# The order of small steps in a two-model transformer kernel: the first norm's weight halves, TensorE's order and VectorE's order at the end of the linear attention

## The reference

```
o_g = o_g * lax.rsqrt(jnp.mean(o_g * o_g, axis=-1, keepdims=True) + EPS)
o_g = o_g.reshape(bsz, seq, GLA_V) * gla_g.astype(F32_2) * jax.nn.silu(gr)
...
mu = jnp.mean(o_r, axis=-1, keepdims=True)
var = jnp.mean(jnp.square(o_r - mu), axis=-1, keepdims=True)
o_r = ((o_r - mu) * lax.rsqrt(var + EPS)).reshape(bsz, seq, RET_V)
o_r = (o_r * gn_g.astype(F32_2) + gn_b.astype(F32_2)) * jax.nn.silu(rg)
o = jnp.concatenate([o_g, o_r], axis=-1).astype(h.dtype)
return o @ w_out
```

## Time and profile before

| | |
|---|---|
| median of 3 runs | 2454.0 us (2450.01 to 2458.52) |
| profiled execution | 2458.52 us, span 2457.1 us |
| TensorE busy | 92% of the span |
| VectorE busy | 65% |
| ScalarE busy | 48% |
| DMA, mean over the span | 174 GB/s |

### The profile page before, as it was taken

The page is one execution under the profiler, slowest core; times in us unless marked ns, Lnnn a source line. Parts: engine busy times, 40 slices in busy tenths (PEclk is TensorE's granted clock), DMA queues, the critical chain, the costliest instruction groups (busy, mean ns, idle before and its releaser), DMA issues.

```text
span 2457.1 us, 44886 instructions
## 1 busy us (share of the span) xinstructions
PE 2270.8 (92%) x19011; PEld 2046.4 (83%) x19011; DVE 1602.9 (65%) x2442; ACT 1174.1 (48%) x1703; POOL 0.2 (0%) x4
## 2 busy tenths in 40 slices
PE   7789788999998888889999989999989999999998
PEld 7469788999976787889998989998988888877776
DVE  6537776688773587666776756555765554477886
ACT  5234534455552354344655435444444443456665
POOL 0000000000000000000000000000000000000000
PEclk9999898999999998989998989999988999999999
DMA  5664333355446542334654425563413554579995
GB/s 206 250 237 157 114 103 112 129 198 194 150 172 240 209 145 86 120 111 139 196 199 137 143 64 179 181 185 135 145 35 111 191 182 181 176 271 324 322 327 194
DMA packets 118634, 427.06 MB, mean 174 GB/s; under 512 B 13344, under 2 KB 16160, under 8 KB 118304
## 3 DMA queue, kind: packets, MB, share of 16 engines
q1 hardware_dynamic: 116016, 421.81, 50.0%
q10 hardware_dynamic: 2416, 2.37, 0.3%
HBM read 423.08 MB, written 1.05 MB: 173 GB/s over the span
## 4 chain that ended last, share of the span: by engine, by line
PE 76%; DVE 15%; ACT 5%; issue 3%; DMA 2%; SPq 0%; ACTq 0%; DVEq 0%
PE bank L801 75%; DVE w_low L2276 4%; DVE arena L2308 4%; DMA ring<-in_weights 2%; DVE arena L2317 1%; ACT w_high L1746 1%; DVE y_mix L2308 1%; DVE arena L2813 1%; PE bank L1631 1%; ACT arena L2025 1%; DVE arena L2312 0%; DVE arena L2314 0%; DVE small L2811 0%; DVE arena L2327 0%; ACT arena L1970 0%
## 5 line engine op out<-in xcount | busy, mean ns | idle before, releaser
L2276 DVE TENSOR_TENSOR w_low<-ring,w_high 128x1024 fp32r<-128x1024 f32 x700 | 822.8, 1219 | 156.6 <-ACT w_high L1746 155.8
L1746 ACT ACTIVATE w_high<-ring 128x1024 fp32r<-128x1024 f32 x700 | 699.8, 1051 | 168.8 <-PE bank L801 159.4
L801 PE MATMUL bank<-u_high,w_high 128*128 128x256 f32 x2576 | 740.2, 287 | 29.7 <-DVE u_low L2308 19.7
L801 PE MATMUL bank<-u_low,w_high 128*128 128x256 f32 x2576 | 731.8, 284 | 0.0
L801 PE MATMUL bank<-u_high,w_low 128*128 128x256 f32 x2576 | 731.4, 284 | 0.0
L801 PEld LDWEIGHTS bank<-u_high,w_high 128*128 128x128 f32 x2576 | 496.6, 193 | 43.8 <-issue 35.5
L801 PEld LDWEIGHTS bank<-u_low,w_high 128*128 128x128 f32 x2576 | 496.4, 193 | 0.1
L801 PEld LDWEIGHTS bank<-u_high,w_low 128*128 128x128 f32 x2576 | 495.4, 192 | 0.0
L801 PE MATMUL bank<-arena 64*64 64x64 f32 (+5 forms) x4456 | 240.5, 251 | 77.6 <-issue 20.8
L801 PEld LDWEIGHTS bank<-arena 64*64 64x64 f32 (+2 forms) x4456 | 210.0, 155 | 115.9 <-issue 62.0
L2308 DVE TENSOR_TENSOR arena<-arena 128x256 f32<-128x256 f32 (+3 forms) x218 | 141.7, 666 | 46.7 <-ACT arena L2069 21.3
(11 more groups left out here) (307 smaller groups left out, 3057.9 us busy)
## 6 DMA issues: line engine op xcount, KB each, us to landing
ring<-in_weights SPq DMA_DIRECT2D x534, 512.0 KB, 4.5
ring<-in_moe SPq DMA_DIRECT2D x264, 512.0 KB, 5.2
const<-in_const SPq DMA_DIRECT2D x1, 2619.0 KB, 16.5
out<-x_res ACTq DMA_DIRECT2D x2, 512.0 KB, 3.0
x_res<-in_x SPq DMA_DIRECT2D x1, 512.0 KB, 5.2
x_res<-in_x ACTq DMA_DIRECT2D x1, 512.0 KB, 5.7
const<-in_par ACTq DMA_DIRECT2D x1, 462.0 KB, 3.4
params<-in_par ACTq DMA_DIRECT2D x1, 247.0 KB, 10.4
```

The lines of the kernel that those rows point to most:

```text
L801: return pe.matmul(out, lhsT, rhs, start=start, stop=stop, skip_group_check=loose)
L1746: act.activation(WH[:, ORDER.slot[cut], :], weights("s", cut), Copy).then_inc(s_hi, 1)
L2276: dve.tensor_tensor(WL[:, b, :], weights("s", cut), WH[:, b, :].bitcast(f32), SUB).then_inc(s_lo, 1)
```

## The change

It has three parts.

1. At the start, ScalarE no longer makes high half 2 between the root and the sigmoid, but behind the sigmoid (the call that follows makes it). VectorE makes low half 1 ahead of the reciprocal instead of behind it, and waits for the parameters there too. Low half 2 stays between the reciprocal and the norm.
2. In the linear attention TensorE spreads the gated heads' roots ahead of `ret_outputs` instead of behind it.
3. In its tail VectorE no longer prepares result times gain times gate and bias times gate ahead of the variance. It multiplies by the spread root, then applies gain and bias in one instruction for each slice, then the gate. The eight instructions that are removed stood ahead of "reps"; four new ones stand behind "rroots", and "mixed0" now comes behind all four products and all four gain-and-bias instructions.

```diff
--- before.py
+++ after.py
@@ -373,15 +373,15 @@
         "normed6 low5 normed7 low6 low7",
     "lin_pe":
         "ga alpha swapped0 sc00 sc01 sc10 sc11 swapped1 turned s0 s1 s2 intra0 intra1 kturned0 y kturned1 rs0 "
-        "rs1 rs2 mean ry roots rmean rvar rroots",
+        "rs1 rs2 mean roots ry rmean rvar rroots",
     "lin_act":
         "-2 soft -1 fades ends kturned0 squares sig -1 root rsig -1 high0 high1 high2 high3 rsquares rroot "
         "high4 high5 high6 high7",
     "lin_dve":
         "ga -1 biased -3 summed end_gap -5 weighted -3 rotated0 -5 masked0 -5 masked1 turned -3 rotated1 -3 "
         "faded -9 state3 -1 intra0 -1 intra1 -1 y -1 kturned1 -11 rstate3 eps -5 inverse -1 ry -3 gated -1 "
-        "centred low0 low1 low2 low3 -9 reps rinverse -1 mixed0 -1 mixed1 low4 -1 mixed2 low5 -1 mixed3 low6 "
-        "low7 x0 x1 x2 x3 x4 x5 x6 x7",
+        "centred low0 low1 low2 low3 -1 reps rinverse -8 mixed0 mixed1 low4 mixed2 low5 mixed3 low6 low7 x0 "
+        "x1 x2 x3 x4 x5 x6 x7",
     "ffn2_pe":
         "sum spread",
     "ffn2_act":
@@ -1519,10 +1519,10 @@
                 ins = mm(psum[1][32 * m:32 * m + 32, 0:T], c_("mean128")[:, 0:32], qn[:, m, :], True, True)
             ins.then_inc(*L.pe.mark("mean"))
             fill(side, 1)
+            pe.wait_ge(*brought(side.jobs[9]))
+            spread_heads(L, qn[:, 0, :])
             pe.wait_ge(*L.dve(f"rstate{NCH - 1}"))
             ret_outputs()
-            pe.wait_ge(*brought(side.jobs[9]))
-            spread_heads(L, qn[:, 0, :])
             fill(side, 1)
             pe.wait_ge(*L.dve("ry"))
             for job in side.jobs[-2:]:
@@ -1793,7 +1793,6 @@
             high_to(1)
             act.wait_ge(*R.pe("sum"))
             act.activation(rstd[:, :], mean_of(R)[:, 0:2], Sqrt, bias=eps).then_inc(*R.act.mark("root"))
-            high_to(2)
             act.wait_ge(s_cond, 16)
             act.activation(small[:, 0:8], cond[:, :], Sigmoid).then_inc(*of_start.act.mark("cond"))
 
@@ -2362,7 +2361,6 @@
             recip(d, rstd[:, :], "inverse")
             if R is of_mix[0]:
                 low_to(2)
-                dve.wait_ge(s_par1, 16)
             dve.wait_ge(*R.pe("spread"))
             for k in range(KT):
                 stt(d, out[:, k, :], X[:, k, :], g_of(k), mean_of(R), MUL, MUL, f"normed{k}")
@@ -3016,13 +3014,6 @@
                 low(L, k, Y)
             dve.wait_ge(*L.act("rsig"))
             tt(d, sg_r, sg_r, rg, MUL)
-            prior(d)
-            dve.wait_ge(*L.act("rsquares"))
-            for m in range(4):
-                stt(d, yr[:, m, :], yr[:, m, :], p2("ret_g", m), sg_r[:, m, :], MUL, MUL)
-            prior(d)
-            for m in range(4):
-                ts(d, sg_r[:, m, :], sg_r[:, m, :], p2("ret_b", m), None, MUL)
             dve.wait_ge(*L.pe("rvar"))
             ts(d, qd[:, 0, :], psum[4][:, 0:T], 1e-6, None, ADD, name="reps")
             dve.wait_ge(*L.act("rroot"))
@@ -3030,8 +3021,12 @@
             dve.wait_ge(*L.pe("rroots"))
             for m in range(4):
                 tt(d, yr[:, m, :], yr[:, m, :], psum[4 + m][:, 0:T], MUL)
-                prior(d)
-                tt(d, yr[:, m, :], yr[:, m, :], sg_r[:, m, :], ADD, f"mixed{m}")
+            prior(d)
+            for m in range(4):
+                ts(d, yr[:, m, :], yr[:, m, :], p2("ret_g", m), p2("ret_b", m), MUL, ADD)
+            prior(d)
+            for m in range(4):
+                tt(d, yr[:, m, :], yr[:, m, :], sg_r[:, m, :], MUL, f"mixed{m}")
                 if m:
                     low(L, 3 + m, Y)
             low(L, KT - 1, Y)
@@ -3188,7 +3183,8 @@
             R, M, A, B, C, G = (d[layer] for d in (of_mix, of_mod, of_a, of_b, of_c, of_merge))
             if layer == 0:
                 first_squares(R)
-                low_to(0)
+                low_to(1)
+                dve.wait_ge(s_par1, 16)
             rms(R, lambda k: par1(layer, "norm_mix", k))
             if layer == 0:
                 dve.wait_ge(*of_start.act("cond"))
```

## The result

The changed kernel took 2478.19 us in the median of five runs (2476.93 to 2488.44), the kernel before 2458.52 us in its five (2450.01 to 2464.2). The ratio is 1.0093, with a 95% interval of 1.0066 to 1.0120. So it is 0.93% slower, some 23 us with 16 to 29 as the bounds, where the forecast was 15.7 us and 0.64%. The two medians of five are 19.7 us apart; all 14 executions of the changed kernel lie between 2472.69 and 2491.84 us. The median lies just above the stated range, which ended at 2478.0. The sign was right and the size too small. The profiled execution took 2472.99 us.

The account below looks back on a forecast made before the run. TensorE, busy 92% of the span, was taken as the bound. Start 1.3, pauses 7.2, tail 2.6 and clock 4.6 summed to 15.7 us, added to 2454.0 for 2469.7 us; range 2458 to 2478.

Parts of the forecast that it names:

- The start's 1.3 us: At the kernel's start, the first normed slice comes 1.3 us later; bounds 0.5 and 2.0.
- The pause ahead of the roots: In each linear attention, TensorE waits 3.61 us for VectorE's reciprocal before spreading the roots; 7.2 us together.
- The tail's pause: TensorE's pause ahead of the tail's last four slices becomes 4.4 us instead of 0.80+2.22.
- the tail's net of 1.3 us: In VectorE's tail, TensorE gets low4 2.15-0.87 = 1.3 us later in each layer; 2.6 us for two.
- the four terms behind rroots: VectorE's tail up to low4: products 1.40, two-scalar instructions 1.37, two products 0.77, wait 0.15; 3.75 instead of 1.6 us.
- the price of that drop: Half-rate clock behind the new pause ahead of the roots: 2.3 us a layer, 4.6 in all; between 0 and 5.1.
- (c): Rival: long clock drops like that of 1422 to 1432, 5.1 us each; 21.3 us in sum, 2475 us; chance 0.12.
- the longer tail pause: Ahead of the tail's last four slices: meets the same clock drop as before, so nothing is added.
- (a): The forecast itself: the pauses and a clock drop in each layer, +15.7 us, 2469.7 us; chance 0.45.
- (b): Rival: the pauses without a new clock drop, 11.1 us, or with one, 13.4; 2465 to 2467 us; chance 0.21.
- (d): Rival: a later wait swallows the pause in TensorE's order; 3.9 us left, 2458 us, no change; chance 0.17.
- (e): Rival: faster, as the shifted program loses low-clock stretches, mainly in the first 1374 us; 2445 us; chance 0.05.

Follow-up runs that it names:

- the tail alone: Only VectorE's tail changed, against the kernel before; ratio 1.0028 (1.0013 to 1.0044).
- the whole change kept busy: The whole change plus unused matmuls in three of TensorE's pauses in each layer; ratio to the kernel before 1.0029 (1.0015 to 1.0043).
- the units first: Kernel before with only TensorE's order changed: roots spread first, then the last two units, then ret_outputs; ratio 1.0056 (1.0037 to 1.0075).
- the order alone: Kernel before with only TensorE's order changed, roots spread ahead of ret_outputs; ratio 1.0080 (1.0060 to 1.0101).
- The two parts' runs: Two runs against the kernel before: only TensorE's order changed, ratio 1.0080, and only VectorE's tail changed, ratio 1.0028.
- with the start: Kernel before with only the start on ScalarE and VectorE changed; ratio 1.0009 (0.9993 to 1.0025).

## Why the prediction was too low

**Right, by its own steps.** The start's 1.3 us were 1.36 at the first matmul, though only 0.7 was left after 240 of them, which the sum did not foresee. The pause ahead of the roots was to be 3.61 us in both layers; it is 3.55. Reps starts directly behind the variance and rroots follow without a pause. The tail's pause was to be 4.4 us; it is 4.42 and 4.41, and the tail's net of 1.3 us is the 1.33 of the run with the tail alone in its second layer. Some of that is luck: the four terms behind rroots add up to 3.69 us and not to the 3.75 that the step gives; 3.78 was measured. The drop of the clock behind the new pause was forecast, and came in both layers.

**Wrong: the price of that drop.** The step reads: "I take the mean of the two that follow pauses, 2.3, twice: 4.6 us." The term measured 4.9 and 4.8 us (A of the changed kernel less A of the whole change kept busy), 9.7 in all where 4.6 was put, near the upper bound of 5.1 a layer and not near the middle. The two rows that it was taken from have large matmuls behind the pause, and with the units first, large matmuls there too, the same pause was followed by 3.4 us at half rate, 1.7 us of cost. Behind the new pause stands ret_outputs, and the nearer row was that of 1422 to 1432. The prediction named exactly this as its rival (c), and gave it 0.12. That choice between two known rows is the failed step. That nearer row shows something more, which the prediction passes over. Windows of the kernel before:

```profile
1417.00:1421.90 4.90, 4.90 (x31) 3.96 (x29) 0.00 (x0) 2.97 (x4) 0.00 (x0) 1.00 0.00 0
1421.90:1432.10 10.20, 10.20 (x43) 9.17 (x43) 4.76 (x6) 1.06 (x1) 0.00 (x0) 0.50 0.21 61
```

The 40 small passes there start at 1417.37, TensorE is busy all the time, its last wait before was 0.69 us ahead of 1408.39, and the clock falls all the same, for 10.2 us, of which the last 5 have large matmuls. So a drop needs no pause right ahead of it. ret_outputs itself, also 40 small passes, ran at 1.00 in the kernel before and met the long drop behind the new pause.

**A second drop had no term.** For the longer tail pause the prediction adds nothing, and that held: C is 0.6 us shorter in the two layers together. (It takes 2.9 and 1.7 us as the cost of the tail's drops before; C against 8.63 gives 2.5 and 1.5.) But in the changed kernel's profile another low stretch, of 3.4 us, lies behind the pause of 2.68 us, in the slices ahead of the variance, in both layers, and costs B 1.5 us each. With the order alone it costs 0.6 us a layer, since TensorE's old wait of 0.80 us ahead of rroots is gone there in exchange. Over all profiles in which these pauses are left unfilled it is in each of the eight layers whose A holds the long drop, and in one of the twelve others, the first layer of the tail alone (the profile of the units first, with 1.81 us there, is one of the runs without it). So it came behind every long drop, and once without one; why, no run here shows.

**The sum as measured.** 0.7 at the start, 7.4 for the pauses ahead of the roots, 2.7 for the tail, 9.7 for the drop behind the new pause; that is 20.5. The remaining 2.3 us of the 22.8 are the balance of the tail's low stretches (+2.9 in B, -0.6 in C), that is again the clock, 12.0 us in all. As for the time itself, 2478.19 is 8.5 us above 2469.7, and 4.5 of these are the base: the sum was added to a median of three, 2454.0, where the five gave 2458.52. The ratio is free of that.

**The rivals.** (c) is what happened: its 21.3 us are the nearest to 23, though it has no term for the second drop either. (a) had the mechanism with too small a price. (b) and (d) fall with the windows above: the drop came and nothing swallowed the pause; the stages behind took as long as before (from the sum of the first layer to the mean of the second, 318.4 us before and 320.1 after). (e) has no support: in the profiled execution the first block was 8.6 us shorter, but the medians show no gain.

**What stays open.** The two parts' runs add up to 1.0117 with the start, above the 1.0093 of the whole though within its interval. Why the pause of 2.68 us is followed by a drop in some executions and not in others isn't settled here, nor why the same work stays at half rate for 3.4 us in one layer and for 6.8 in another. Whether the first block's scatter of several us comes wholly from where its low stretches fall wasn't tested.

## What to carry to other kernels

An independent step that stands ahead of a wait on a nearly saturated TensorE is cover: before it is moved behind the wait, look up when the awaited result is ready, and count the difference as a pause. Price the pause with the clock, by a row of the trace that has the same kind of work behind the pause and not only the same pause, and keep the longest such row as a bound. Where a pause can't be avoided, matmuls whose result nobody uses are worth more than nothing, if they end before the awaited result arrives; covering only part of the pause may give back nothing. And work removed from an engine's queue ahead of a wait is a gain only down to the next thing that arrives there: here 2.8 us of VectorE's work were worth 0.9.

## What the runs showed of the hardware

A pause of 2.00 us ahead of ret_outputs cost as much as one of 3.55: the granted clock went to 0.50, that is 1.2 GHz, for 10.2 us in both cases, while in the same place with large matmuls behind the pause it was low for 3.4 us. TensorE counts as busy for those 10 us (10.00 of 10.00 in the window from 1815 in the second layer), so the busy share doesn't show the loss; the clock column does. The Trainium skill (TensorE: Matmul & The Clock Gate, section HAM oscillation — how this bites in real kernels) says that a TensorE which waits for its operands again and again falls back to half rate and starts each next stretch of work slow. The traces agree for the new pause, in all eight layers that have ret_outputs behind it. They don't behind the pause ahead of the output projection's first slice (2.68 us, 1.81 with the units first), where the clock stayed at 1.00 in 11 of 20 layers. And at 1421.9 it fell with no wait ahead. The Trainium skill (ScalarE: Activation LUTs, section What ACT_TABLE_LOAD costs) gives a switch a drain of 1.38 us beside the load of 1.28. The load agrees. The drain isn't in the trace: the changed kernel's load begins at 11.48, 0.02 us behind the end of the root, and its sigmoid at 12.78, 0.02 us behind the end of the load.
